# Gate projections in sixteen chunks between the jobs of attention and the pair products, with a new order of the projections ahead of them

## What is computed

```python
h = rmsnorm(x, ln1)
proj = h @ w_in                       # 1536 columns q, k, v; 1792 recurrent; 2048 gates
q, k, v = split(proj[..., :1536])
rc      = proj[..., 1536:3328]
gates   = proj[..., 3328:]
o_a = attend(q, k, v)                 # dilated window attention, bias by distance
xr  = rc + (prev(rc) - rc) * rwkv_mu  # token shift, then decay, keys, a, g from xr
o_b = rwkv7(xr)                       # delta-rule state update
gate_a, gate_b = split(gates, 2)
mixed = sigmoid(gate_a) * (o_a @ w_branch_a) + sigmoid(gate_b) * (o_b @ w_branch_b)
x = x + mixed @ w_out
x = x + moe(rmsnorm(x, ln2))          # top 4 of 32 experts
```

## Time and profile before

| | us |
|---|---|
| median of 3 executions | 1394.12 (1393.66 to 1395.07) |
| profiled execution, its time | 1392.25 |
| profiled execution, first to last instruction | 1390.5 |
| TensorE busy | 1298.7 (93%) |
| VectorE / ScalarE / GpSimd busy | 380.9 / 258.6 / 73.9 |
| DMA, mean over the span | 331 GB/s |

### The profile page before, as it was taken

The page is one execution under the profiler, slowest core; times in us unless marked ns, Lnnn a source line. Parts: engine busy times, 40 slices in busy tenths (PEclk is TensorE's granted clock), DMA queues, the critical chain, the costliest instruction groups (busy, mean ns, idle before and its releaser), DMA issues.

```text
span 1390.5 us, 16932 instructions
## 1 busy us (share of the span) xinstructions
PE 1298.7 (93%) x6700; PEld 629.5 (45%) x6700; DVE 380.9 (27%) x706; ACT 258.6 (19%) x469; POOL 73.9 (5%) x44
## 2 busy tenths in 40 slices
PE   5999968898889999999999999999999999999995
PEld 5887855797745333333333333333333333333331
DVE  3042765965553111211121112111121111111113
ACT  2112424113202211111111111111111111111112
POOL 0000161360000000000000000000000000000000
PEclk9999989899897999999999999999999999999998
DMA  7356664013448799999999999999999999999993
GB/s 264 139 154 164 213 203 103 1 40 131 156 154 376 281 424 429 428 429 428 428 430 428 429 427 429 428 428 429 429 427 429 429 428 429 427 429 428 429 428 146
DMA packets 52200, 459.93 MB, mean 331 GB/s; under 512 B 7882, under 2 KB 10260, under 8 KB 27580
## 3 DMA queue, kind: packets, MB, share of 16 engines
q1 hardware_dynamic: 48676, 450.41, 78.6%
q0 software_dynamic: 1888, 5.34, 2.0%
q10 hardware_dynamic: 1600, 3.69, 0.8%
HBM read 454.27 MB, written 5.11 MB: 330 GB/s over the span
## 4 chain that ended last, share of the span: by engine, by line
PE 70%; DMA 18%; DVE 5%; issue 3%; ACT 2%; POOL 1%; SPq 1%; ACTq 0%; DVEq 0%; POOLq 0%
PE ps L1662 23%; PE ps L1690 13%; DMA work<-in_w_gate_up 10%; PE ps L1265 8%; DMA ring<-in_w_gate_up 7%; PE ps L1603 4%; PE ps L1647 3%; PE ps L1618 3%; PE ps L1397 3%; PE ps L1525 2%; PE ps L1240 1%; PE ps L1610 1%; DVE ring L805 1%; PE ps L1466 1%; ACT work L690 1%
## 5 line engine op out<-in xcount | busy, mean ns | idle before, releaser
L1662 PE MATMUL ps<-ring,work 128*64 128x512 f32 x1536 | 337.1, 593 | 8.9 <-DMA ring<-in_w_gate_up 7.9
L1662 PEld LDWEIGHTS ps<-ring,work 128*64 128x64 f32 x1536 | 109.6, 137 | 230.5 <-issue 211.5
L1690 PE MATMUL ps<-ring,work 128*64 128x512 f32 x768 | 170.1, 595 | 0.0
L1265 PE MATMUL ps<-work,ring 128*128 128x264 f32 x672 | 150.3, 386 | 0.5 <-DVE work L805 0.5
L1265 PEld LDWEIGHTS ps<-work,ring 128*128 128x128 f32 x672 | 127.5, 190 | 22.3 <-DVE work L805 0.6
L1178 DVE TENSOR_SCALAR work<-ps 128x512 f32<-128x512 f32 x32 | 22.1, 692 | 406.9 <-PE ps L1662 406.9
L1196 DVE SCALAR_TENSOR_TENSOR work<-work 128x512 f32<-128x512 f32 x32 | 24.0, 751 | 373.9 <-ACT work L722 373.9
L1662 PE MATMUL ps<-work 128*64 128x512 f32 x512 | 113.5, 593 | 3.3 <-DMA work<-in_w_gate_up 3.3
L1690 PEld LDWEIGHTS ps<-ring,work 128*64 128x64 f32 x768 | 53.0, 137 | 115.4 <-issue 115.4
L713 ACT ACTIVATE work<-work 128x512 f32<-128x512 f32 x32 | 20.1, 630 | 416.3 <-DVE work L1178 416.3
L805 DVE TENSOR_TENSOR work<-work 128x512 f32<-128x512 f32 (+8 forms) x78 | 62.7, 804 | 51.0 <-ACT work L509 45.0
(11 more groups left out here) (256 smaller groups left out, 1052.9 us busy)
## 6 DMA issues: line engine op xcount, KB each, us to landing
ring<-in_w_gate_up SPq DMA_DIRECT2D x96, 2048.0 KB, 25.6
ring<-in_w_down SPq DMA_DIRECT2D x48, 2048.0 KB, 31.1
work<-in_w_gate_up SPq DMA_DIRECT2D x32, 2048.0 KB, 27.3
work<-in_w_down SPq DMA_DIRECT2D x16, 2048.0 KB, 31.1
ring<-in_w_in SPq DMA_DIRECT2D x6, 3072.0 KB, 16.3
ring<-in_w_out SPq DMA_DIRECT2D x1, 4096.0 KB, 14.3
ring<-in_w_in SPq DMA_DIRECT2D x2, 1536.0 KB, 9.9
ring<-in_cache_k SPq DMA_DIRECT2D x16, 192.0 KB, 3.2
```

The lines of the kernel that those rows point to most:

```text
L1265: last = mm(psum(job, T), WIN[gi % 2][:, k, j * 128:(j + 1) * 128], hT[:, k, :], start=k == 0, stop=k == KD - 1)
L1662: last = mm(PS[bnk][g * 64:g * 64 + 64, :], lhs, UNIT[n % 8][:, w0 + base + g * 512:w0 + base + (g + 1) * 512], start=False, stop=k == KD - 1)
L1690: last = mm(PS[BY][g * 64:g * 64 + 64, :], lhs, UNIT[n % 8][:, w0:w0 + 512], start=k == 0, stop=k == KD - 1)
```

## The change

- Entry: one root is taken ahead of the data, each tile's root directly follows its square, and the ln1 rows are loaded right behind the identity and transposed alone (`ln1T`). ScalarE copies the second half of each `hT` tile out with ln1 as its scale. The rest of `par` and `ssT` is transposed after chunk 17.
- Order of chunks: 12 to 25, 0 to 4, then `lw`, `la`, `lg`, `nk`, `qn`, 5 to 7, `kn`, 8 to 11, `vn`. The weights come in five loads (`LOADS`). `bvp` and `bvs` stand after chunk 23; `sh` is copied out by ScalarE.
- The sixteen gate chunks are jobs `gc0` to `gc15`: two behind scores 0 and 1, one behind `pt` of each head, one behind each half of `decode`, one behind each of the first four kinds of pair products. Their weights come in pieces of 512 KB into four small buffers `WG`, two loaded by SyncE, the others by ScalarE when a chunk is copied out. They are copied out without a function; two late sigmoids on 8 chunks each follow the A2 copies.
- VectorE takes the `nk` maxima ahead of the decay scan, score 0 ahead of all key sums, and the key sums between heads 0 to 3; `sst` and `spt` come one head later.
- `pairs` alternates the two halves of 64 rows at every matmul.

```diff
-    jobs += pr(2, 3, 4) + ["bvp", "bvs"] + [f"sh{g}" for g in range(4)] + pr(0)
...
+    pr = lambda a, b: [f"pr{n}" for n in range(a, b)]
+    jobs = ["ln1T"] + [f"hT{m}{g}" for m in range(NM) for g in range(2)]
+    jobs += pr(12, 18) + ["par", "ssT"] + pr(18, 24) + ["bvp", "bvs"] + pr(24, 26) + [f"sh{g}" for g in range(4)] + pr(0, 5)
+    jobs += [f"lw{c}" for c in range(4)] + [f"la{c}" for c in range(4)] + [f"lg{c}" for c in range(4)] + [f"nk{c}" for c in range(4)]
+    jobs += ["qn"] + pr(5, 8) + [f"kn{m}" for m in range(NM)] + pr(8, 12) + [f"vn{m}" for m in range(NM)] + ["s0", "s1", "gc0", "gc1"]
...
+LOADS = ((12, 6), (18, 6), (24, 2), (0, 6), (6, 6))
+GBUF = (0, 1, 2, 3, 0, 1, 2, 3, 2, 3, 2, 3, 2, 3, 2, 3)
...
-            for i in range(2, 7):
-                wait_pe(f"pr{GROUPS[i - 2] * GC + GC - 1}")
+            for n in range(2):
+                load(WG[n], gate_columns(n), f"ld_wg{n}")
+            for i in range(2, 5):
+                first, n = LOADS[i - 2]
+                wait_pe(f"pr{first + n - 1}")
                 load_win(i)
...
+            A_(nc.scalar.activation(rs1[:1, 0:1], eps[:1], ACT.Sqrt))
             for m in range(NM):
...
+                A_.ready(nc.scalar.activation(rs1[:n, m:m + 1], sq1[:n, m:m + 1], ACT.Sqrt, bias=eps[:n], scale=1.0 / D), "rms1", m + 1)
+                if m == 0:
+                    evacuate("ln1T", parT[:, P_LN1:P_LN1 + 8], psum("ln1T", 8))
...
+                for c in range(4):
+                    ins = nc.scalar.activation(hT[:, 4 + c, m * 128:m * 128 + n], psum(job, 4, n)[:, c], ACT.Copy,
+                                               scale=parT[:, P_LN1 + 4 + c:P_LN1 + 5 + c])
...
+            def load_gate(n):
+                act.dma_start(WG[GBUF[n]], gate_columns(n)).then_inc(S_(f"ld_wg{GBUF[n]}"), 16)
+
+            def gate_chunk(n):
+
+                evacuate(f"gc{n}", sgT[:, n, :], psum(f"gc{n}", T))
+                later = [i for i in range(n + 1, CG) if GBUF[i] == GBUF[n]]
+                if later:
+                    load_gate(later[0])
...
+            gate_chunk(0)
+            gate_chunk(1)
+            act.wait_ge(S_("rk"), 1)
+            load_gate(2)
+            load_gate(3)
             exponents(0)
...
                 evacuate(f"pt{h}", ptb[:, h % 2, :], psum(f"pt{h}", 384))
+                gate_chunk(h + 2)
...
+            for n in range(2):
+                v = sgT[:, n * KD:(n + 1) * KD, :]
+                A_.ready(nc.scalar.activation(v, v, ACT.Sigmoid), "gates", n + 1)
...
-            for b in range(5):
-                reduce_b(b)
             score(0)
+            reduce_b(0)
...
                 if h < 3:
-                    reduce_b(5 + h)
-                if h == 4:
+                    reduce_b(2 * h + 1)
+                    reduce_b(2 * h + 2)
+                if h == 3:
+                    reduce_b(7)
...
                 pe.wait_ge(S_("pn"), h + 1)
                 transposes(f"pt{h}", [ssb[:, h % 2, 128 * t:128 * t + 128] for t in range(3)], 128)
+                gate_chunk(h + 2)
...
+            pairs("Auk", kbar, kt)
+            gate_chunk(12)
+            pairs("Brk", kbar, rt)
+            gate_chunk(13)
+            pairs("Aub", bbar, kt)
+            gate_chunk(14)
+            pairs("Brb", bbar, rt)
+            gate_chunk(15)
+            pairs("A8", kt, bbar)
```

More of the change, by code:

```diff
@@ L1241, in transposes @@
                 done(last, job)
[L1243 to L1247 removed]
+            pe.wait_ge(S_("ld_ident"), 32)
+            transposes("ln1T", [par[P_LN1:P_LN1 + 8, :]], 8)
             for m in range(NM):
@@ L1268, in _, with project @@
-            project(2, 3, 4)
+            after(pe, *[f"hT{m}{g}" for m in range(NM) for g in range(2)])
+            def project(*chunks):
+                for n in chunks:
+                    i = [l for l, (first, count) in enumerate(LOADS) if first <= n < first + count][0]
+                    j = n - LOADS[i][0]
+                    if i and j == 0:
+                        pe.wait_ge(S_(f"ld_win_{i % 2}"), 16 * ((i + 1) // 2))
+                    elif i == 0 and j % 3 == 0:
+                        pe.wait_ge(S_("ld_win0" + "ab"[j // 3]), 16)
+                    job = f"pr{n}"
+                    give(job)
+                    for k in range(KD):
+                        last = mm(psum(job, T), WIN[i % 2][:, k, j * 128:(j + 1) * 128], hT[:, k, :], start=k == 0, stop=k == KD - 1)
+                    done(last, job)
@@ new lines, in gate_chunk @@
+            def gate_chunk(n):
+                pe.wait_ge(S_(f"ld_wg{GBUF[n]}"), 16 * (GBUF[:n].count(GBUF[n]) + 1))
+                job = f"gc{n}"
+                give(job)
+                for k in range(KD):
+                    last = mm(psum(job, T), WG[GBUF[n]][:, k, :], hT[:, k, :], start=k == 0, stop=k == KD - 1)
+                done(last, job)
+            project(*range(12, 18))
+            pe.wait_ge(S_("ld_par"), 16 * 8)
+            transposes("par", [par[:P_N, :]], P_N)
+            pe.wait_ge(S_("ld_ss"), 16)
@@ L1269, in _ @@
+            transposes("ssT", [ss[:NB, c * 128:(c + 1) * 128] for c in range(CR)], NB)
+            project(*range(18, 24))
             pe.wait_ge(S_("ld_mats"), 16)
```

225 lines of the change are left out of this document (107 added, 118 removed).

## The result

The changed kernel takes 1400.17 us (median of 9 executions, 1394.51 to 1407.08) against 1394.27 us for the kernel before, run on the same chip (9 executions, 1388.76 to 1398.12): a ratio of 1.0058, 95% interval 1.0039 to 1.0076. It is slower by 5.9 us where 8.6 us less had been predicted, and outside the range of 1371 to 1397. The difference is small (0.6%), but its interval lies clear of no change. Its profiled execution took 1407.01 (span 1405.2), one of the longest of the nine.

A forecast was written before the change was run, and what follows sets the result against it. TensorE's own work ahead of the first A2 product was taken as what counts: 14.2 + 127.7 + 87 + 24.8 = 253.7 against 262.3, -8.6, so 1385.5 us from a median of 1394.12; range 1371 to 1397.

The forecast's parts named there:

- Entry: Start of the kernel up to the first projection: from 20.8 to about 14.2 us, bounds 13.2 to 15.5.
- Front stream: Projections between entry and attention: from 168.9 to about 127.7 us, including a 9.2 us hole and 2.0 of lower clock.
- R1: Rival: the load for chunks 0 to 5 lands in 10.1 us, hidden, without hole or clock loss; 1374 us, chance 20%.
- the sigmoid table, 1.28: Between chunk 4 and the tanh TensorE waits for: the sigmoid table load adds 1.28 us to the 1.50 there.
- Attention: Attention with twelve gate chunks: from 53.2 to about 87 us, floor 73.2 plus named waits of 13.3.
- the first wait: Start of attention: TensorE waits 3 us for late exponents of head 0, and 1.5 more for gate chunk 2's weights.
- 7 us or more of cover: In attention, the 512 KB gate-weight loads have at least 7 us of cover and go beside the V loads.
- R3: Rival: gate chunks stand in attention's serial chain and hide nothing; attention 95.9, pairs 33.6, 17.7 more, 1403 us, chance 12%.
- rule of sign: R3 decides where less than 9.2 of the 57 us moved are hidden, since 47.8 are won ahead of attention.
- Pairs: Pair products with four gate chunks: from 19.4 to about 24.8 us, between estimates set by TensorE and by VectorE's masks.
- Behind it: After the pair products: late sigmoid pushes A2T copies by 5.7 us yet just fits; cost 0, bounds 0 and +2.
- that part keeps its length: From the first A2 product on, two thirds of the run: unchanged length, so an earlier start passes through one to one.

The follow-up runs named there:

- e1: Changed kernel with both bias products, and so the bias-row store, moved from behind chunk 23 to behind chunk 4: 1403.8 us, ratio to before 1.0070.
- e14: e12 without the early sigmoid: 1389.6 us, ratio to before 0.9969.
- e5: Changed kernel with third to fifth weight loads recut (24, 25, 0 to 3; 4, 5; 6 to 11): 1391.5 us, ratio to before 0.9981.
- e6: Changed kernel plus a one-element sigmoid on ScalarE behind the copies of the last tokens: 1393.9 us (one execution).
- e12: e9 with the last two loads even (chunks 4 to 7, 8 to 11) and sample-query loads sent behind chunk 7: 1382.6 us, ratio to before 0.9929.
- e4: Changed kernel with the products of the cached keys on VectorE instead of GpSimd: 1407.6 us.
- e3: Changed kernel with gate chunks 2 to 9 doing only the first of their eight products: 1396.6 us (one execution).
- e2: Kernel before with only the change's entry (ln1 first, early root, split copies, par and ssT between projections): 1392.0 us, ratio 0.9973.
- e9: Changed kernel with the edits of e5 and e6 together: 1395.6 us, ratio to before 1.0023.

## Why the prediction was wrong, step by step

**Entry:** 14.75 and 14.6 for a forecast of 14.2; right. The twelve copies took 4.41 instead of 3.5.

**Front stream:** 133.05 for 127.7. The hole was named with its cause and size (9.77 for 9.2), and e1 shows the cause. R1's price for it (11.2 less without it) stands beside 10.2: e14, which starts chunk 0 from an earlier load, is 4.3 us under the kernel before, the changed kernel 5.9 over. The step that failed first is the term "the sigmoid table, 1.28": that tanh comes first and loads a set of its own was not seen. The idle time is 4.06 instead of 2.8. The three waits for evacuations were 0.74 each instead of 0.45. Together with the hole that is 2.7 us more of idle time than in the sum.

Another 2.7 us are TensorE's busy time. Behind the hole 0.8 us more are lost than the 2.0 in the sum (five chunks in 20.72 us, 17.97 where there is no hole, as in e5), and par with ssT takes 1.2 instead of 1.9. The rest is in the first six chunks: they take 23.9 us in the changed kernel (23.4 in the second profile) and 21.3 in the profile that the sum started from. In their first four microseconds they make 5 and 6 matmul records in 2 us, later 11; the granted clock reads 1.00 throughout, so the rows don't say why. The second profile of the kernel before has some of it too (eighteen chunks in 66.08 us, 64.32 in the first). With the lora products (the low-rank products `lw`, `la` and `lg`) it is the other way round. They take 8.32 us in the changed kernel and just as long in that first profile, behind an idle time of only 1.5, so the slow clock was in the base of the sum by chance. In the two later profiles of the kernel before it is not there; the second:

```profile
19.25 66.08 PE L1265 MATMUL ps<-work,ring 128*128 128x264 f32 x288 [0.40 <-DVE work L805]
...
111.24 4.99 PE L1284 MATMUL ps<-work 64*128 64x264 f32 x24 [1.50 <-issue]
```

So the change does cost 3.3 us there against most executions of the kernel before, by the odds under e6, and the sum had no term for it. In whole times the one table costs 5.8 us (e12 and e14), where 1.3 were in the sum.

**Attention:** 96.4 and 90.2 for 87. The waits of heads 1 to 3 came as forecast (5.64 and 5.66 in all for 5.3). Three terms were too small. One is the first wait, 7.34 and 6.62 for 4.5 (3 and 1.5 in the sum). VectorE's chain from the norms of the keys is 40.2 us long instead of "some 35":

```profile
115.94 1.83 DVE L892 TENSOR_SCALAR work<-ps 128x264 f32<-128x264 f32 x4 [30.16 <-PE ps L1339]
...
155.42 0.70 DVE L949 MEMSET ring<- 128x768 f32 x1 [0.23 <-DVE work L850]
```

Its two multiplications met GpSimd's first products, which the earlier kn had moved to just there. I had counted this lock for the scalings of the heads and not for the chain ahead of them. In e4, where GpSimd makes no products, the same chain takes 35.2 us. But the first wait is 5.50 there and not 4.5, so without the lock, in the chain and in head 0's scaling (2.07 for 0.30), the wait is only 1.8 us shorter; what is left ends with the exponents, as said under e4. The second term is the lower clock: TensorE is busy for 78.45 and 77.02 us, where the sum had 73.2 and 2. A gate chunk takes 3.73 us at full clock and up to 5.51 behind a wait. The third is "7 us or more of cover" for the gate weights. It didn't hold for chunk 8 in the first profile, where a load took 11.7 us beside the cached values: the very point that the prediction had named as one that would make it wrong. In the second profile the load was in time. So this term is between 0 and 4, and which of the two a profile shows is chance.

**R3** was the rival with the right sign, but not the right mechanism. The chunks do hide: a third to a half of their work in e3, and the pair products with all four are 5.7 us longer for 14.2 to 15.3 of work. R3 also expected 33.6 us for the pairs, which took 25.1. Its own rule of sign, set against what was really won ahead of attention, comes out both ways: 41.9 of the 57 us moved were won there, so 15.1 had to be hidden, and the first profile hid 8.1. In the second 43.2 were won and 14.3 hidden, and A2 is 0.5 us earlier than before.

**Pairs:** 25.1 for 24.8; right, but TensorE sets this stage (25.05 busy) and not the mean of two limits. Its matmuls take 2.06 / 16 = 0.129 us instead of 0.154 (at a granted clock of 1.00 both times), and the chunks 3.8 instead of 3.56. So the four chunks cost 5.7 us here net of what the alternating halves save, some 2 us for 80 matmuls (estimate from 0.025 each).

**Behind it:** the late sigmoid fits, as forecast. It ends its copies of A2T at 281.6, and the products of A4 start at 285.2, 7.0 later than before like A2 itself. What failed is the sentence "that part keeps its length" at the head of the prediction. Between the first A2 product and the expert stage it varied by 8.5 us in two executions of e2 and by 10.5 over all profiles, so that one profile of each kernel can't be read to better than that, and it may be longer by the change as well.

In sum: entry 0.5, front 5.35, attention 9.4 and pairs 0.3 bring A2 from 253.7 to 269.3 in the first profile; 0.4, 4.2, 3.2 and 0.3 bring it to 261.8 in the second. The second profile is the nearer one to the medians: its span is 6.5 us over the first one of the kernel before, the medians differ by 5.9. Of the 15.1 us that it lies over the forecast, 8.1 stand ahead of A2 and 7.0 behind it, and for the latter the cause stays open.

## What to carry to other kernels

When a load loses its cover, don't only price the wait: list every transfer that will be in flight with it, and ask the same for the next load, which the fix will uncover (e1, e9). A function moved away may have been the one that brought its neighbour's table in; look at the order of the table loads after the move. A hole ahead of dense matmuls can cost more than its length: 2.56 us of idle time less gave 4.2 us at the first A2 product and 5.8 in the whole (e12, e14). And start a sum from more than one profile. The base of this one had a slow stretch that most executions lack and lacked one that others have, and behind A2 it was near the short end.

## What the runs showed of the hardware

- Sigmoid's table set serves tanh, but tanh alone brings in another; each load takes 1.28 us (e6, changed kernel).
- Behind 1.50 us of idle time the lora products took 4.99 us in nine of eleven profiles, behind 4.06 us 8.30 to 9.45 in all eight, at a granted clock down to 0.50.
- The store of the bias rows (1.5 MB) takes 35 to 37 us wherever it is put. Loads of 3 MB beside it landed after 20.9, 29.7 and 37.1 us, against 10.1 alone; a store of 16 KB held its waiter up for 17 us (e1).
- Beside a GpSimd product a scaling of VectorE took 3.53 us instead of 0.35, and five copies of 32 columns 6.59 instead of 1.05 (e12); a product on VectorE itself takes 1.76.
- The same instructions between the w_branch products and the gathers took 117.0 and 123.8 us in two executions of one kernel. Of the 6.8 us between them 6.5 are TensorE's busy time (109.0 against 102.5), at a granted clock of 0.84 and 0.82 against 0.89 and 0.86.
